# Computing 56 of 96 modulation blocks of a two-model block stack on VectorE instead of TensorE

## The chip, the cores and the metric

The kernel runs on one core of a Trainium2 chip. The metric is the device time in microseconds of one execution; every input and output is float32, and all weights (some 340 MB in one execution) come from HBM. TensorE multiplies, VectorE and ScalarE work element by element, GpSimd helps and starts some transfers, and SyncE's queue starts the loads of the weight stream. In the trace these are PE (with PEld, its weight loads), DVE, ACT, POOL and SP.

## The reference, cut to what matters

The reference is a stack of two layers with adaptive normalisation, followed by a third block (a long convolution, a gated recurrence and a retrieval of experts) that the change doesn't touch. There are 256 tokens of the latent and 256 of the context, width 1024. Each of the two layers begins from modulations, one vector of six times 1024 for the latent's condition and one for the context's:

```python
for i in range(DEPTH):                      # DEPTH = 2
    last = i == DEPTH - 1
    m_lat = (silu(c) @ ada_w[i] + ada_b[i])[:, None, :]     # ada_w[i]: 1024 x 6144
    m_ctx = silu(c_ctx) @ ada_w[i] + ada_b[i]
    sh1, sc1, g1, sh2, sc2, g2 = split(m_lat, 6)
    csh1, csc1, cg1, csh2, csc2, cg2 = split(m_ctx, 6)
    h  = rms(x, norm1_g[i]) * (1 + sc1) + sh1
    hc = rms(y, norm1_g[i]) * (1 + csc1) + csh1
    o, oc = mixer(h, hc)                    # layer 0: Fourier and window attention; layer 1: neighbourhood attention
    x = x + g1 * o
    x = x + g2 * swiglu(rms(x, norm2_g[i]) * (1 + sc2) + sh2)
    if not last:
        y = y + cg1 * oc
        y = y + cg2 * swiglu(rms(y, norm2_g[i]) * (1 + csc2) + csh2)
```

In the last layer the context's rows g1, sh2, sc2 and g2 are used by nothing.

## The kernel before

**The weight stream.** All weights are one list of blocks of 128 x 1024 floats (0.524 MB), in the order in which they are used (`STREAM`). SyncE's queue loads them in that order into a ring of six places (`RING`); a load waits until the block that held its place before is used up. The two 1024 x 6144 matrices of the modulations are 96 such blocks: `ada0a` (16), `ada0b` (32), `ada1a` (16), `ada1b` (32).

**Modulations on TensorE.** `ada` (line 737, its matmul is line 743) takes one block: 128 of the 1024 inputs by 1024 outputs. The condition's column, padded to 32 columns, is the stationary operand and the weight the moving one, in two halves of 512, on 32-column strips of the array, so that the two blocks of a group run side by side. The sums lie in two banks as rows; `ada_copy` (ScalarE) copies them out, and `ada_turn` (TensorE, line 757) turns them into columns with sixteen small matmuls; `mods` (VectorE) adds the bias and forms the gains.

**Where they stand.** `ada0a` opens the program, because the first norm needs it. The others fill TensorE's program elsewhere: `fill[0]`, 48 blocks (`ada0b` and `ada1a`), of which 18 stand between the Fourier steps and 30 in attention 0, two after the scores of each pair; `fill[1]`, 32 blocks (`ada1b`), two after the scores of each of the 16 pairs of attention 1. The turns stand behind the first tile of `ev_out` and of `od_out`, the projections that follow the two attentions.

**An attention** goes over 16 pairs of heads (a pair: two heads, one tile of 128 queries). In step i TensorE's program has scores of pair i (line 949), the two filling blocks, values of pair i-3 (line 970), turning of the probabilities of pair i-2 (line 958). VectorE takes the row minima (`row_min`, line 2168, one instruction that adds the mask and keeps the minimum), ScalarE the exponentials of pair i (line 1593) and behind them in its program the copies of the turned probabilities of pair i-2 (line 1601), GpSimd scales the probabilities (line 2896). Attention 0 has pairs of 512 and of 256 keys, two and two in turn; attention 1 has 512 throughout. In attention 0 GpSimd also splits the four Fourier rows, ahead of its pairs 4 to 7.

**A projection** multiplies in three terms. Each weight block is split in a high part (ScalarE, `high`, line 1612) and a low part (VectorE, `low`, line 2029), both kept in three places (`PARTS`); TensorE does 24 matmuls of 128 x 512 for a tile (line 998). In `ffn`, gate and up tiles alternate: ScalarE applies Silu to gate tile 2m, VectorE multiplies with up tile 2m+1, copies the product's high part and subtracts for its low part. Tile 2m+3 starts once that product has freed its bank (three banks in turn). VectorE's program in step m: low part of block 2m+3, product of pair m, low part of block 2m+4. In `residual` (the end of `ev_out` and `od_out`) VectorE's low parts and residual sums alternate with ScalarE's squares and high parts.

## Time and profile before

| | |
|---|---|
| median of 3 runs | 2174.22 us (2173.36 to 2176.29) |
| the profiled execution | 2173.93 us, its span 2172.1 us |
| TensorE busy | 2100.5 us, 97% of the span |
| VectorE busy | 1399.0 us, 64% |
| ScalarE busy | 973.6 us, 45% |
| GpSimd busy | 321.2 us, 15% |
| matmuls of the modulations (line 743) | 64.9 us busy |
| weight stream | 618 loads of 512 KB by SyncE's queue |

Shares of busy time are averages over stages that have different limits, and a busy TensorE is not one at its peak: its matmuls are pipelined and their ends are modelled. What a stage is bound by is read from the chain of work that ended last (which engine each stretch of the end's history belongs to) and from the timeline of the stage: an engine whose rows stand end to end is the limit there, and a bracket at a row's end names what the engine waited for before it.

### The profile page before, as it was taken

The page shows a single profiled execution, that of the slowest core. Times are in us where ns is not written, and L with a number is a line of the kernel's source. Part 1 is how long each engine was busy: PE and PEld are TensorE (multiplying, and loading weights), DVE is VectorE, ACT ScalarE, POOL GpSimd, SP SyncE. Part 2 cuts the span into 40 slices and gives each one's busy share as a digit, 9 for nine tenths or more (in the row PEclk, how much of TensorE's full clock was granted, in tenths as well). Part 3 has the DMA queues.
Part 4 walks back from the last instruction along what each step waited for, and adds up shares of the span by engine and source line. Part 5 has one row for each costly group of instructions (what it writes and reads, how often), then busy time and mean ns, then how long its engine had stood idle before and what let it go on. Part 6 is the DMA issues. An engine that isn't in the chain of part 4 may idle for free.

```text
span 2172.1 us, 35323 instructions
## 1 busy us (share of the span) xinstructions
PE 2100.5 (97%) x12873; PEld 1777.2 (82%) x12873; DVE 1399.0 (64%) x2524; ACT 973.6 (45%) x1544; POOL 321.2 (15%) x339
## 2 busy tenths in 40 slices
PE   5999999999999999899999999999999999999998
PEld 2754778888878757899999988999988888888887
DVE  4435454443238845665587867997996677777776
ACT  3426332222234345444458635446743444444444
POOL 0014000000003022000000005787840000000000
PEclk9999999999999999999999999999999999999999
DMA  7348322222226356455544634552246655555553
GB/s 287 117 165 312 106 70 97 97 97 97 97 78 175 106 176 205 154 182 183 186 152 175 211 121 140 168 184 68 68 156 219 193 194 187 190 187 192 186 191 116
DMA packets 92751, 341.14 MB, mean 157 GB/s; under 512 B 10367, under 2 KB 10383, under 8 KB 92256
## 3 DMA queue, kind: packets, MB, share of 16 engines
q1 hardware_dynamic: 89280, 325.10, 44.6%
q0 software_dynamic: 3360, 14.51, 2.3%
q8 instruction: 76, 1.25, 0.2%
q14 instruction: 35, 0.29, 0.0%
HBM read 338.52 MB, written 1.05 MB: 156 GB/s over the span
## 4 chain that ended last, share of the span: by engine, by line
PE 89%; DVE 5%; ACT 3%; issue 1%; DMA 1%; SPq 0%; POOL 0%; DVEq 0%; ACTq 0%
PE banks L998 21%; PE banks L1438 16%; PE banks L1047 8%; PE banks L1404 7%; PE banks L1316 6%; PE banks L1187 5%; PE banks L1407 3%; PE banks L1365 3%; PE banks L743 2%; PE banks L923 2%; PE banks L1349 2%; PE banks L1085 2%; PE banks L949 1%; PE banks L970 1%; DMA weight_ring<-in_stream 1%
## 5 line engine op out<-in xcount | busy, mean ns | idle before, releaser
L998 PE MATMUL banks<-act_parts,first_w_parts 128*128 128x512 f32 (+1 forms) x2592 | 477.7, 345 | 7.2 <-DMA small_zone<-in_smalls 3.4
L998 PEld LDWEIGHTS banks<-act_parts,first_w_parts 128*128 128x128 f32 x2592 | 410.4, 190 | 71.0 <-issue 5.6
L2029 DVE TENSOR_TENSOR first_w_parts<-weight_ring,first_w_parts 128x1024 fp32r<-128x1024 f32 x166 | 206.7, 1248 | 263.1 <-ACT first_w_parts L1612 263.1
L1438 PE MATMUL banks<-w_parts,a_parts 128*128 128x512 f32 x1524 | 360.4, 390 | 0.1
L1438 PEld LDWEIGHTS banks<-w_parts,a_parts 128*128 128x128 f32 x1524 | 285.9, 188 | 59.4 <-issue 0.8
L1612 ACT ACTIVATE w_parts<-weight_ring 128x1024 fp32r<-128x1024 f32 x207 | 218.9, 1058 | 184.0 <-PE banks L1404 102.0
L2029 DVE TENSOR_TENSOR w_parts<-weight_ring,w_parts 128x1024 fp32r<-128x1024 f32 x207 | 253.6, 1226 | 72.0 <-ACT w_parts L1612 71.8
L1612 ACT ACTIVATE first_w_parts<-weight_ring 128x1024 fp32r<-128x1024 f32 x166 | 174.7, 1057 | 237.4 <-PE banks L998 125.7
L1404 PE MATMUL banks<-n_parts,w_parts 128*128 128x512 f32 x632 | 229.4, 397 | 1.3 <-DVE w_parts L2029 1.3
L1047 PE MATMUL banks<-ffn_hidden_parts,first_w_parts 128*128 128x512 f32 (+1 forms) x1056 | 183.4, 336 | 0.0
L1047 PEld LDWEIGHTS banks<-ffn_hidden_parts,first_w_parts 128*128 128x128 f32 x1056 | 162.5, 190 | 20.6
L1407 PE MATMUL banks<-n_parts,w_parts 128*128 128x256 f32 x632 | 164.3, 281 | 0.0
L1404 PEld LDWEIGHTS banks<-n_parts,w_parts 128*128 128x128 f32 x632 | 118.6, 188 | 26.8 <-DVE w_parts L2029 1.6
L2029 DVE TENSOR_TENSOR banks<-banks,main_zone 128x256 f32<-128x256 f32 (+1 forms) x174 | 97.7, 565 | 53.4 <-ACT main_zone L1953 52.7
L1407 PEld LDWEIGHTS banks<-n_parts,w_parts 128*128 128x128 f32 x632 | 119.5, 189 | 6.1
L1187 PE MATMUL banks<-n_parts,mix_w_parts 128*128 128x256 f32 (+1 forms) x1008 | 123.2, 284 | 0.5 <-DVE mix_w_parts L2029 0.5
L1187 PEld LDWEIGHTS banks<-n_parts,mix_w_parts 128*128 128x128 f32 x1008 | 122.5, 188 | 0.7 <-DVE mix_w_parts L2029 0.7
L1316 PE MATMUL banks<-n_parts,query_w_parts 128*128 128x256 f32 x888 | 109.9, 284 | 1.9 <-POOL query_w_parts L2934 1.9
L1316 PEld LDWEIGHTS banks<-n_parts,query_w_parts 128*128 128x128 f32 x888 | 107.7, 192 | 2.4 <-POOL query_w_parts L2934 2.3
L2934 POOL TENSOR_TENSOR query_w_parts<-weight_ring,query_w_parts 128x1024 fp32r<-128x1024 f32 x41 | 99.0, 2418 | 51.2 <-ACT query_w_parts L1612 31.4
L2029 DVE TENSOR_TENSOR mix_w_parts<-weight_ring,mix_w_parts 128x1024 fp32r<-128x1024 f32 x59 | 72.0, 1223 | 36.5 <-ACT mix_w_parts L1612 36.1
L1953 ACT ACTIVATE main_zone<-banks 128x256 f32<-128x256 f32 x79 | 30.3, 384 | 124.3 <-PE banks L1404 124.3
(310 smaller groups left out, 2866.5 us busy)
## 6 DMA issues: line engine op xcount, KB each, us to landing
weight_ring<-in_stream SPq DMA_DIRECT2D x618, 512.0 KB, 3.3
main_zone<-in_rel_bias POOLq DMA_DIRECT2D x6, 512.0 KB, 10.9
rounded<-in_dft_input POOLq DMA_DIRECT2D x1, 1600.0 KB, 8.6
rounded<-in_dft_inverse POOLq DMA_DIRECT2D x1, 1280.0 KB, 6.1
main_zone<-in_xT POOLq DMA_DIRECT2D x1, 1024.0 KB, 12.1
main_zone<-in_ctxT POOLq DMA_DIRECT2D x1, 1024.0 KB, 16.9
tail_zone<-in_rel_bias POOLq DMA_DIRECT2D x2, 512.0 KB, 23.7
main_zone<-in_keysT POOLq DMA_DIRECT2D x1, 1024.0 KB, 8.9
```

The lines of the kernel that those rows point to most:

```text
L743: mm = pe.matmul(bank[ADA_BANKS[phase][half]][strip:strip + 32, :], cond[:, k, 10 - 2 * row:42 - 2 * row], wb[:, half * 512:(half + 1) * 512],
L998: mm = pe.matmul(o[:, 0:w], wb[:, hw, k, :], fin[:, hx, k, 0:w], start=(k == 0 and n == 0), stop=(k == DC - 1 and n == 2))
L1047: mm = pe.matmul(o[:, 0:w], wb[:, hw, b % 8, :], fhid[:, hx, k, 0:w], start=(k == 0 and n == 0), stop=(k == FC - 1 and n == 2))
L1187: mm = pe.matmul(o[:, cols], wb[:, hw, k, :], n0p[:, hx, k, cols], start=(k == 0 and n == 0), stop=(k == DC - 1 and n == 2))
L1316: mm = pe.matmul(o[:, 0:L], wb[:, hw, k, :], rows[:, hx, k, :], start=(k == 0 and n == 0), stop=(k == DC - 1 and n == 2))
L1365: mm = pe.matmul(twins[h][:, j * P:(j + 1) * P], one1[:, 8 * h + j, :], one2[:, 8 * h + j, :], start=True, stop=True)
L1404: return pe.matmul(o[:, :], w[:, 0, k, :], n2p[:, :, k, :], start=(k == 0), stop=(k == DC - 1))
L1407: return pe.matmul(o[:, 0:L], w[:, 1, k, :], n2p[:, 0, k, :], start=False, stop=False)
L1438: mm = pe.matmul(acc[n][:, :], ap_[:, e % 3, ha, (n // 2) * P:(n // 2 + 1) * P], wp[(B + b) % PARTS][:, hw, (n % 2) * 512:(n % 2 + 1) * 51 ...
L1612: act.activation(parts[n % PARTS][:, 0, :], slot(s), ACT.Copy).then_inc(w_hi, 1)
L2029: return dve.tensor_tensor(o, a, b, op)
L2934: pool.tensor_tensor(w[:, 1, :], slot(s), w[:, 0, :].bitcast(F32), ALU.subtract).then_inc(w_lo, 1)
```

## The change

`ada0a` stays. `ada0b` is cut to 24 blocks (the rows g1, sh2 and sc2 of layer 0), which stay filling on TensorE: 18 between the Fourier steps and six in the first three pairs of attention 0. The other 56 blocks, row g2 of layer 0 and all of layer 1, become `mods`: each is laid out with the output channel on the partition and all 1024 inputs along the row, and VectorE multiplies it with a row of the condition that is the same on every partition and sums, one instruction for each block and sample (`mod_sums`). The first 24 blocks have two samples (latent and context), the other 32, whose context rows nobody uses, only the latent: 80 instructions. They are woven into the first feed-forward: two blocks in each of the gate and up pairs 1 to 12, five in 13 to 16, four in 17 to 19, one or two (or three) behind each low part, and their blocks stand at the same places of the weight stream. The condition's rows are loaded by GpSimd's queue behind `ev_out`, and ScalarE applies Silu to them behind its first gate tile. The products themselves go to a bank pair that nobody reads. `late_mods` adds biases and forms the gains at the end of gate and up. The turn, the copies and the modulation step of the old `ada1b` are gone.

```diff
-STREAM = [("ada0a", 16), ("ev_in", 10), ("ada0b", 32), ("ada1a", 16), ("ev_out", 8), ("ffn_gu0", 2 * FC), ("ffn_d0", FC),
-          ("od_in", 24), ("ada1b", 32), ("od_out", 8), ("ffn_gu1", 2 * FC), ("ffn_d1", FC),
+STREAM = [("ada0a", 16), ("ev_in", 10), ("ada0b", 24), ("ev_out", 8), ("ffn_gu0", 2 * FC), ("mods", 56), ("ffn_d0", FC),
+          ("od_in", 24), ("od_out", 8), ("ffn_gu1", 2 * FC), ("ffn_d1", FC),
...
+MODS = ([(0, 5, _j, 2) for _j in range(8)] + [(1, _r, _j, 2) for _r in range(2) for _j in range(8)]
+        + [(1, _r, _j, 1) for _r in range(2, 6) for _j in range(8)])
...
+        _c = 1 if _m < 13 else 2 + (_part == 1 and _m < 17)
+        MODS_AT[_m, _part] = range(_at, _at + _c)
...
+                if name == "mods":
+                    return mod_used, n + 1
...
-                nj = [2, 6, 4][phase]
+                nj = [2, 3][phase]
...
-            fill = [[(1, name, b, row0 + b // DC, row0 + b // DC == 0, row0 + b // DC == 5)
-                     for name, n, row0 in (("ada0b", 32, 0), ("ada1a", 16, 4)) for b in range(n)],
-                    [(2, "ada1b", b, b // DC, b // DC == 0, b // DC == 3) for b in range(32)]]
+            fill = [[(1, "ada0b", b, b // DC, b // DC == 0, b // DC == 2) for b in range(24)], []]
...
-                if m == 0:
-                    ada_turn(2)
...
+                    if l == 0 and m == 0:
+                        act.wait_ge(crow_in, 16)
+                        for s in range(2):
+                            act.activation(c_rows[:, s, :], c_rows[:, s, :], ACT.Silu).then_inc(crow_ready, 1)
...
-            ada_copy(2)
...
+            def mod_sums(blocks):
+
+                for b in blocks:
+                    l, row, m, samples = MODS[b]
+                    s = SLOTS["mods"][b]
+                    dve.wait_ge(landed[PLACE[s]], 16 * LOADS[s])
+                    for n in range(samples):
+                        if b == 0:
+                            dve.wait_ge(crow_ready, 2 - n)
+                        last = dve.tensor_tensor_reduce(out=twins[3][:, :], in0=slot(s), in1=c_rows[:, 1 - n, :], scale=1.0, scalar=0.0,
+                                                        op0=ALU.mult, op1=ALU.add, accum_out=MOD[:, l, 8 * row + m, n:n + 1])
+                        if n < samples - 1:
+                            link(last)
+                    last.then_inc(mod_used, 1)
+                    dve.wait_ge(mod_used, b + 1)
...
+                    if l == 0:
+                        mod_sums(MODS_AT.get((m, 0), ()))
                     p = tile(name, 2 * m + 1)[:, 0:w]
...
+                    if l == 0:
+                        mod_sums(MODS_AT.get((m, 1), ()))
+                if l == 0:
+                    late_mods()
...
-            mods(0, 1)
-            mods(1, 0)
+            mods()
             residual("ev_out", 0, 16, T)
...
-            mods(1, 1)
             residual("od_out", 1, 16, L)
...
+            pool.wait_ge(tile_ready, TILE["ev_out"] + 8)
+            pool.dma_start(view(CROWS0, 2 * D), t["c_rows"][:, :]).then_inc(crow_in, 16)
```

What stands in a row on the engines follows, in the line numbers of each kernel. On TensorE in attention 1, a step in the middle before (scores, filling, values, turning of the probabilities):

```order
L949 MATMUL banks<-main_zone 128x512 x2
L743 MATMUL banks<-weight_ring,small_zone 32x512 x4
L970 MATMUL banks<-tail_zone,main_zone 64x128 x8
L958 MATMUL banks<-small_zone,tail_zone 128x128 x8
L949 MATMUL banks<-main_zone 128x512 x2
```

and after:

```order
L968 MATMUL banks<-main_zone 128x512 x2
L989 MATMUL banks<-tail_zone,main_zone 64x128 x8
L977 MATMUL banks<-small_zone,tail_zone 128x128 x8
L968 MATMUL banks<-main_zone 128x512 x2
L989 MATMUL banks<-tail_zone,main_zone 64x128 x8
```

The filling between scores and values is gone; the rest stands in the same order.

On VectorE in gate and up of layer 0, one step before (low part, product, its high and low part, low part):

```order
L2029 TENSOR_TENSOR first_w_parts<-weight_ring,first_w_parts 128x1024 [waits weight_high_parts] x2
L2029 TENSOR_TENSOR banks<-tail_zone,banks 128x512 [waits silu_ready,tile_ready]
L2275 CAST ffn_hidden_parts<-banks 128x512 [waits dve_chain]
L2029 TENSOR_TENSOR ffn_hidden_parts<-banks,ffn_hidden_parts 128x512 [waits dve_chain]
L2029 TENSOR_TENSOR first_w_parts<-weight_ring,first_w_parts 128x1024 [waits weight_high_parts] x2
```

and after, in pair 2 (the instruction of line 2114 multiplies and sums; the short one behind it reads the sum):

```order
L2049 TENSOR_TENSOR first_w_parts<-weight_ring,first_w_parts 128x1024 [waits weight_high_parts,modulation_rows_summed]
L2114 ISA banks,small_zone<-weight_ring,main_zone 128x1024 [waits weights_landed2]
L2114 ISA small_zone 128x1
L2114 ISA banks,small_zone<-weight_ring,main_zone 128x1024 [waits dve_chain]
L2114 ISA small_zone 128x1
L2049 TENSOR_TENSOR banks<-tail_zone,banks 128x512 [waits silu_ready,tile_ready,modulation_rows_summed]
L2323 CAST ffn_hidden_parts<-banks 128x512 [waits dve_chain]
L2049 TENSOR_TENSOR ffn_hidden_parts<-banks,ffn_hidden_parts 128x512 [waits dve_chain]
L2049 TENSOR_TENSOR first_w_parts<-weight_ring,first_w_parts 128x1024 [waits weight_high_parts]
```

Behind each low part stand one block's sums now, and the product waits behind them.

On VectorE at the start of `od_out`, before (low part of block 1, the last modulations, low part of block 2, first residual):

```order
L2029 TENSOR_TENSOR act_parts<-weight_ring,act_parts 128x8x128 [waits weight_high_parts]
L2029 TENSOR_TENSOR small_zone<-banks,small_zone 128x64 [waits ada_ready]
L2022 TENSOR_SCALAR small_zone<-small_zone 128x16 [waits dve_chain]
L2029 TENSOR_TENSOR small_zone<-small_zone 128x16 [waits dve_chain]
L2029 TENSOR_TENSOR unused_query_columns<-weight_ring,unused_query_columns 128x8x128 [waits weight_high_parts,dve_chain]
L2026 SCALAR_TENSOR_TENSOR main_zone<-banks,small_zone,main_zone 128x256 [waits tile_ready]
```

and after (with the last values' high and low part ahead of it):

```order
L2262 CAST act_parts<-banks 128x128 [waits attention_out_ready]
L2049 TENSOR_TENSOR act_parts<-banks,act_parts 128x128 [waits attention_out_high_parts]
L2049 TENSOR_TENSOR act_parts<-weight_ring,act_parts 128x8x128 [waits weight_high_parts]
L2049 TENSOR_TENSOR unused_query_columns<-weight_ring,unused_query_columns 128x8x128 [waits weight_high_parts]
L2046 SCALAR_TENSOR_TENSOR main_zone<-banks,small_zone,main_zone 128x256 [waits tile_ready]
```

The three modulation steps and their wait for the turn have left the place ahead of the low part of block 2.

## Rows read from the trace of the kernel before

**Rows 1.** The page's chain of work that ended last, shares by engine

```profile
PE 89%; DVE 5%; ACT 3%; issue 1%; DMA 1%; SPq 0%; POOL 0%; DVEq 0%; ACTq 0%
```

**Rows 2.** The chain in order of time, gate and up of layer 0: start, us, what

```profile
291.35 228.48 PE banks L998 x1008
```

**Rows 3.** Timeline, TensorE, attention 1: start, us, engine, line, operation, idle before

```profile
786.82 2.08 PE L743 MATMUL banks<-weight_ring,small_zone 128*32 128x512 f32 x8
...
807.29 1.13 PE L949 MATMUL banks<-main_zone 64*128 64x512 f32 x4
808.35 1.06 PE L743 MATMUL banks<-weight_ring,small_zone 128*32 128x512 f32 x8
809.34 1.09 PE L970 MATMUL banks<-tail_zone,main_zone 128*64 128x128 f32 x16
...
811.39 1.13 PE L949 MATMUL banks<-main_zone 64*128 64x512 f32 x4
```

**Rows 4.** Timeline, all engines, same pair: exponentials, then copies of pair i-2

```profile
809.77 0.72 ACT L1593 ACTIVATE tail_zone<-tail_zone,small_zone 128x512 f32<-128x512 f32 x1 [1.62 <-DVE small_zone L2168]
...
811.20 1.05 ACT L1601 ACTIVATE tail_zone<-banks 128x512 f32<-128x512 f32 x2
```

**Rows 5.** Timeline, TensorE, attention 0: a filling, its second half, scores

```profile
168.09 1.05 PE L743 MATMUL banks<-weight_ring,small_zone 128*32 128x512 f32 x4
169.44 1.05 PE L743 MATMUL banks<-weight_ring,small_zone 128*32 128x512 f32 x4 [0.29 <-DMA weight_ring<-in_stream]
...
172.47 1.13 PE L949 MATMUL banks<-main_zone 64*128 64x512 f32 x4
...
187.57 1.13 PE L949 MATMUL banks<-main_zone 64*128 64x512 f32 x4
...
201.44 1.13 PE L949 MATMUL banks<-main_zone 64*128 64x512 f32 x4
```

**Rows 6.** Timeline, all engines, attention 0

```profile
184.37 1.28 POOL L2890 TENSOR_TENSOR act_parts<-main_zone,act_parts 128x512 fp32r<-128x512 f32 x1
...
191.24 1.13 PE L949 MATMUL banks<-main_zone 64*128 64x512 f32 x4
...
194.47 0.70 PE L949 MATMUL banks<-main_zone 64*128 64x256 f32 x4
...
194.79 0.64 ACT L1601 ACTIVATE tail_zone<-banks 128x256 f32<-128x256 f32 x2
...
196.38 0.49 ACT L1593 ACTIVATE tail_zone<-tail_zone,small_zone 128x257 f32<-128x257 f32 x1
```

**Rows 7.** Timeline, start of the od_out stage

```profile
851.54 1.85 PE L757 MATMUL banks<-small_zone,main_zone 128*128 128x8 f32 x16
...
855.25 0.48 DVE L2026 SCALAR_TENSOR_TENSOR main_zone<-banks,small_zone,main_zone 128x256 f32<-128x256 f32 x1
...
858.30 0.48 DVE L2026 SCALAR_TENSOR_TENSOR main_zone<-banks,small_zone,main_zone 128x256 f32<-128x256 f32 x1
```

**Rows 8.** Timeline, start of gate and up of layer 0

```profile
291.20 2.00 ACT L1612 ACTIVATE first_w_parts<-weight_ring 128x1024 fp32r<-128x1024 f32 x2
292.29 1.23 DVE L2029 TENSOR_TENSOR first_w_parts<-weight_ring,first_w_parts 128x1024 fp32r<-128x1024 f32 x1 [5.61 <-ACT first_w_parts L1612]
293.43 0.69 DVE L2029 TENSOR_TENSOR banks<-tail_zone,banks 128x512 f32<-128x512 f32 x1
...
295.55 1.22 DVE L2029 TENSOR_TENSOR first_w_parts<-weight_ring,first_w_parts 128x1024 fp32r<-128x1024 f32 x1
```

**Rows 9.** Groups by line and shape, attention 0: shapes, count | busy, mean ns

```profile
L2168 DVE CUSTOM_DVE_ANT_0 tail_zone<-banks,main_zone,small_zone 128x512 f32<-128x512 f32 x12 | 8.9, 747 | 0.0
...
L2168 DVE CUSTOM_DVE_ANT_0 tail_zone<-banks,main_zone,small_zone 128x256 f32<-128x256 f32 x16 | 7.6, 478 | 0.0
```

**Rows 10.** Timeline, VectorE in the norm ahead of gate and up of layer 1

```profile
882.41 0.48 DVE L2026 SCALAR_TENSOR_TENSOR act_parts<-main_zone,small_zone,act_parts 128x256 fp32r<-128x256 f32 x1
```

**Rows 11.** Stretches, attention 0: us; busy by engine; granted clock, DMA share, GB/s

```profile
170.00:175.00 5.00, 5.00 (x48) 2.65 (x46) 1.88 (x7) 1.52 (x3) 0.32 (x1) 1.00 0.98 373
```

More of the change, by code:

```diff
@@ L67 @@
           ("peer", 2 * KEYS - DONE)]
-SLOT = {}
+MODS = ([(0, 5, _j, 2) for _j in range(8)] + [(1, _r, _j, 2) for _r in range(2) for _j in range(8)]
+        + [(1, _r, _j, 1) for _r in range(2, 6) for _j in range(8)])
+MODS_AT = {}
 _at = 0
-for _n, _c in STREAM:
-    SLOT[_n] = _at
-    _at += _c
-NSLOTS = _at
+for _m in range(1, 20):
+    for _part in range(2):
+        _c = 1 if _m < 13 else 2 + (_part == 1 and _m < 17)
+        MODS_AT[_m, _part] = range(_at, _at + _c)
+        _at += _c
+assert _at == len(MODS)
+ORDER = []
+for _n, _c in STREAM:
+    for _i in range(_c if _n != "mods" else 0):
+        ORDER.append((_n, _i))
+        if _n == "ffn_gu0" and _i >= 3:
+            ORDER += [("mods", _b) for _b in MODS_AT.get(((_i - 3) // 2, (_i - 3) % 2), ())]
+SLOTS = {_n: [] for _n, _ in STREAM}
+for _s, (_n, _i) in enumerate(ORDER):
+    SLOTS[_n].append(_s)
+SLOT = {_n: _s[0] for _n, _s in SLOTS.items()}
+NSLOTS = len(ORDER)
 SPLIT = ("ev_in", "ev_out", "ffn_gu0", "ffn_d0", "od_in", "od_out", "ffn_gu1", "ffn_d1", "w_in2a", "w_in2b", "w_in2c", "w_in2d",
@@ L79 @@
 KIND = []
-_n = [0, 0]
-for _name, _c in STREAM:
-    _k = _name in SPLIT
-    ORD[_name] = _n[_k]
-    for _i in range(_c):
-        KIND.append((_k, _n[_k], _name, _i))
-        _n[_k] += 1
+_n = [0, 0, 0]
+for _name, _i in ORDER:
+    _k = 2 if _name == "mods" else int(_name in SPLIT)
+    ORD.setdefault(_name, _n[_k])
+    KIND.append((_k, _n[_k], _name, _i))
+    _n[_k] += 1
 EARLY_QUERIES = 4
@@ L237, in ada_strip @@
     return (2 * k + k // 4 % 2) % 4 ^ half
+CROWS0 = 21504
 HALF0 = FS0 + 2048
@@ L3112, in layout @@
         ada = x["ada_w"][l].reshape(DC, P, 6, 1024).transpose(2, 0, 1, 3).reshape(48, P, 1024)
-        parts[f"ada{l}a"], parts[f"ada{l}b"] = ada[:16], ada[16:]
+        if l == 0:
+            parts["ada0a"], parts["ada0b"] = ada[:16], ada[16:40]
         parts[f"ffn_gu{l}"] = woven(tiled(x["ffn_w_gate"][l]), tiled(x["ffn_w_up"][l]))
         parts[f"ffn_d{l}"] = tiled(x["ffn_w_down"][l])
+    parts["mods"] = np.stack([x["ada_w"][l][:, D * row + P * m:D * row + P * (m + 1)].T for l, row, m, _ in MODS])
     stream = np.empty((NSLOTS, P, 1024), np.float32)
```

47 lines of the change are left out of this document (29 added, 18 removed).

## The prediction

> **What bounds the kernel now.** I read the chain of work that ended last first: 89% of it is TensorE, the rest short stretches of VectorE, ScalarE and DMA [rows 1]. So an edit pays only where it shortens TensorE's program, or a stretch where TensorE waits. The first gate and up projection is TensorE alone: 42 tiles in one unbroken piece, 228.48/42 = 5.44 us a tile [rows 2]. In the two attentions TensorE's own timeline shows, for every pair of heads, scores, the two modulation blocks as filling, values of three pairs ago, turning of two pairs ago, with nothing between [rows 3]. There too TensorE is the bound, but what the filling hides has to be looked up: in the timeline of all engines, ScalarE starts the exponentials 2.48 us after the scores start and ends the copies of the turned probabilities 4.96 us after [rows 3, 4]. Those are on no path today, and are next when the filling goes.
>
> **Removed: the filling of attention 1** (32 blocks, two in each of 16 pairs). A pair takes 811.39 - 807.29 = 4.10 us, of which the filling is 809.34 - 808.35 = 0.99 [rows 3]. Without it TensorE alone would need 3.11. But values of pair i-2, which stand in pair i+1, need the copies of pair i-2, and ScalarE does these behind the exponentials of pair i. Count from scores i: copies done at +4.96 [rows 4], about +0.09 for the semaphore (estimate), then values and turning, 811.39 - 809.34 = 2.05 [rows 3], and after them come scores i+2. Two pairs per 7.10 us are 3.55 a pair. The gain is therefore 0.55 of the 0.99, in the 13 pairs from the fourth on: 7.1 us. The first three have no values to do, their scores wait for VectorE's minima, and I give them nothing. One filling there took 2.08 where the others take 1.06 [rows 3], because its weights were late: another 1.0. Sum 8.1 us. Ends: 13 x 0.99 + 1.0 = 13.9 if ScalarE kept up, and 1.0 if the chain took all of it back.
>
> **Removed: the filling of attention 0 from the fourth pair on** (24 of 30 blocks; pairs 0 to 2 keep theirs). Sizes alternate there, two pairs of 512 keys, two of 256, so I take rounds of four: 201.44 - 187.57 = 13.87 us [rows 5]. The same reasoning, with this attention's offsets: after scores of 512 keys the copies start at 194.79 - 191.24 = +3.55, after scores of 256 at 196.38 + 0.49 - 194.47 = +2.40; copies of 256 take 0.64 [rows 6], of 512 1.05 [rows 4]; values and turning take about 0.59 each for 256 (estimate: half of 1.03 and a fixed part). Following the even pairs: (3.55 + 0.64 + 0.08 + 0.59 + 0.59) + (2.40 + 1.05 + 0.08 + 1.03 + 1.02) = 11.0; the odd ones: (3.55 + 0.64 + 0.08 + 0.59 + 1.02) + 5.36 (TensorE's own work there) = 11.2. The slower sets it: 13.87 - 11.2 = 2.65 a round, and 12 fillings are three rounds: 8.0 us. Late weights go as well: the filling that began at 168.09 should have let the next scores start at 168.09 + 1.0 + 2.05 = 171.1, and they started at 172.47, its second half having waited for a DMA: 1.3; the round behind it took 187.57 - 172.47 = 15.10, 1.2 over the clean one [rows 5]. Against this GpSimd splits the Fourier rows in pairs 4 to 7, one subtraction of 1.28 and more for each [rows 6]; at the new pace it is nearly full, and I charge 0.5 (between 0 and 1.3). Sum 10.0 us. Ends: 12 x 1.0 + 2.5 = 14.5, and 2.5.
>
> **Removed: the turn of the last modulations in the od_out stage.** VectorE there waits for tile 0, then for TensorE's sixteen small matmuls of the turn (they start at 851.54, where tile 0 ends), then does three links and a weight's low part before the first residual at 855.25 [rows 7]. From there a ladder of VectorE and ScalarE runs, 858.30 - 855.25 = 3.05 us a step, longer than TensorE's tile; whoever starts the ladder earlier ends it earlier. With the turn gone the low part needs nothing new and is done while tile 0 runs, and the residual can start 0.14 behind 851.54: 855.25 - 851.68 = 3.6; I take 3.5. In the ev_out stage the turn stays, TensorE is the bound, and the three links that leave VectorE there are worth nothing.
>
> **Added: 80 multiply-and-sum instructions on VectorE in the gate and up projection.** 24 blocks have two samples and 32 one. The form, both inputs in SBUF and 1024 long, is in no row. The nearest are the attention's row minima, the same instruction with one input in PSUM: 0.478 us for 256, 0.747 for 512 [rows 9], so 0.269 for each further 256, and 0.747 + 2 x 0.269 = 1.28 for 1024. With reading the sum and waiting for itself I take 1.35 apart (estimate). Per gate-and-up pair VectorE does today two low parts at 293.43 - 292.29 = 1.14 and three steps of the product, 295.55 - 293.43 = 2.12 [rows 8]: 4.4 of TensorE's 10.88. Pairs 1 to 12 get four sums: 4.4 + 5.4 = 9.8. Pairs 13 to 16 get five: 11.15, which is 0.27 too long, four times 1.1. Pairs 17 to 19 have four again. What stands behind a late sum on VectorE is the next product; TensorE's tile 2m+3 needs its bank one tile after that product's input is ready, so it can be 5.44 - 2.1 - 0.1 = 3.2 late. 1.1 is below this: cost 0. From the fixed parts, the sums begin to cost at (10.88 - 4.4)/4 = 1.62 apart.
>
> **Added on the other queues.** ScalarE gets two Silu of 1024 before the high part of block 3. Its rows of that size take 1.0 each [rows 8]. That block's low part stands ahead of the first product on VectorE, which now ends near 297.7 instead of 295.6, and tile 3 would start at 291.2 + 5.44 = 296.6: cost 1.1, once, and 0 to 3. SP loads 100 blocks instead of 44 through the same six places; the densest stretch is seven in 10.88 us, 7 x 0.524 MB/10.88 = 337 GB/s, and five microseconds of attention 0 moved 373 [rows 11]. It fits, without much left; cost 0, at worst a few us. The row load of the condition is on GpSimd's queue, which has nothing else there. The seven small links at the end of the projection lie ahead of low parts that are three blocks early.
>
> **The sum.** 10.0 + 8.1 + 3.5 - 1.1 = 20.5 us. The profiled execution took 2173.93; 2173.93 - 20.5 = 2153.4. The median of the runs is 0.3 above the profiled one: 2153.7.
>
> **A rule against it.** The row that bears on the price is a scalar-tensor-tensor with both inputs in SBUF, 256 long and without a sum: 0.48 us [rows 10], as long as the minima of that length, so two SBUF inputs alone halve nothing here. The Trainium skill, Vector Engine (DVE) Microarchitecture Reference, section 7 "Points that are easy to get wrong", says of a related instruction form that two SBUF sources wider than bf16 halve its throughput, because no read port is left for the accumulator. No run here shows a form that both sums and reads twice from SBUF, so it stands as a rival.
>
> **Rivals.**
> - The sums run at half rate. Slope doubled, 0.21 + 4 x 0.54 = 2.36, and 2.43 apart. Then VectorE bounds the projection: 4.4 + 9.7 = 14.1 in fifteen pairs (3.2 over) and 16.6 in four (5.7 over), 48 + 23 - 3 = 68 us. 2153.7 + 68 = 2222, slower. It decides from about 1.83 apart, where the loss, 60 x (1.83 - 1.62) + 20 x (1.83 - 1.30) - 3.2, eats the 20.5. For it: no row shows the form. Against: the row above. 0.12.
> - The sums are somewhat dearer, 1.65 to 1.8 apart, or weights come late where seven blocks share a pair: 5 to 18 us back, 2159 to 2172. 0.11.
> - ScalarE's chain does not bind: attentions fall to TensorE's own pace, 13.9 + 14.5 + 3.5 - 1.1 = 30.8: 2143. Against: its copies stand behind the exponentials in program order. 0.07.
> - The change does little: the chains take the filling's time back, only stalls and the turn are left, 1.0 + 2.5 + 3.5 - 1.1 = 5.9: 2168. Against it: ScalarE's own work in a pair, from the first exponential to the last copy, is 812.25 - 809.77 = 2.48 [rows 4], far from 4.10. 0.04.
> - My forecast, 2147 to 2160: 0.66.
>
> **How the numbers follow.** A measurement of this kernel can tell about 0.2%, 4.3 us, from no change. The range 2143 to 2172 takes in all but the half rate and tails, some 0.16. Faster by over 0.2% (below 2169.9): the forecast, the better case, and most of the dearer sums and of the little-gain case, 0.80. Within 0.2%: 0.06. Slower: the half rate and worse mishaps, 0.14.
>
> **What would show it.** The sums' row: 1.28 confirms the price, above 1.6 fails it. The projection's TensorE piece: unbroken but for a gap of about 1 us at tile 3. In attention 1, scores alternating at about 3.1 and 4.0 us with TensorE waiting for ScalarE's copies; regular 3.1 would make the second attention's term too small, 4.1 none at all. In the od_out stage the first residual right behind tile 0. The forecast is wrong if VectorE is busy all through the projection while TensorE waits for its low parts or banks.

## The result, and the profile after

The changed kernel takes 2157.18 us (median of four runs, 2156.76 to 2157.65) where the kernel before, on the same chip, takes 2173.86 (2173.36 to 2176.29): a ratio of 0.9924, 95% interval 0.9911 to 0.9938. The profiled execution took 2157.02, its span 2155.2. The forecast was 2153.7 with 2143 to 2172, and faster. Profile against profile the gain is 16.9 us where 20.5 was forecast. I take it apart by stage, each from TensorE's first matmul in it to its first in the next; the columns are the kernel before, the changed one, the difference and the forecast term.

| stage | before | after | difference | forecast |
|---|---|---|---|---|
| start to attention 0 | 159.96 | 158.34 | -1.6 | none |
| attention 0 | 61.18 | 51.95 | -9.2 | -10.0 |
| ev_out | 55.17 | 55.17 | 0 | 0 |
| gate and up, layer 0 | 243.36 | 244.53 | +1.2 | +1.1 |
| down, layer 0 | 119.77 | 119.77 | 0 | 0 |
| norm, od_in, values' rows | 137.89 | 138.91 | +1.0 | 0 |
| attention 1 | 71.23 | 64.91 | -6.3 | -8.1 |
| od_out and its norm | 33.68 | 31.90 | -1.8 | -3.5 |
| the rest | 1289.86 | 1289.72 | -0.1 | 0 |

(The gate and up projection is 0.16 us longer, in both, if counted to the start of the next piece in the chain, as the expectations below do.)

The page's chain by engine answers [rows 1]; TensorE's share is 88% where it was 89%, ScalarE's 4% where it was 3%.

```profile
PE 88%; DVE 5%; ACT 4%; issue 2%; DMA 1%; POOL 0%; SPq 0%; DVEq 0%; ACTq 0%
```

**Gate and up** first. The chain in order of time (start, us, what) answers [rows 2] and [rows 8]:

```profile
281.31 1.05 ACT main_zone L1659
282.36 0.96 ACT first_w_parts L1629
...
283.37 1.11 issue
...
284.48 0.70 DVE banks L2049
...
286.00 0.70 DVE ffn_hidden_parts L2049
...
286.83 223.32 PE banks L1017 x984
```

The second Silu of the condition (L1659), block 3's high part, its low part (VectorE runs it in the 1.11 us that the chain calls issue), the product: then tile 3, for which TensorE waited 0.89 us, and from there TensorE is unbroken for 223.32 us. The sums are one row of the page (busy us, mean ns of one | idle before):

```profile
L2114 DVE CUSTOM_DVE_ANT_0 banks<-weight_ring,main_zone 128x1024 f32<-128x1024 f32 x80 | 98.4, 1230 | 1.4
```

1.23 us each, 98.4 us of VectorE's time, and the only place where they show in the stage's length is that Silu.

**Attention 1.** TensorE's timeline (start, us, engine, line, operation, idle before) at its start and in the steady part answers [rows 3]:

```profile
768.67 1.13 PE L968 MATMUL banks<-main_zone 64*128 64x512 f32 x4 [0.78 <-ACT main_zone L1591]
...
771.18 2.42 PE L968 MATMUL banks<-main_zone 64*128 64x512 f32 x4 [1.38 <-DVE small_zone L2214]
...
774.53 2.48 PE L968 MATMUL banks<-main_zone 64*128 64x512 f32 x4 [0.93 <-DVE small_zone L2214]
...
776.94 1.83 PE L977 MATMUL banks<-small_zone,tail_zone 128*128 128x128 f32 x8
...
778.70 1.13 PE L968 MATMUL banks<-main_zone 64*128 64x512 f32 x4
...
796.64 1.13 PE L968 MATMUL banks<-main_zone 64*128 64x512 f32 x4
...
801.67 1.09 PE L989 MATMUL banks<-tail_zone,main_zone 128*64 128x128 f32 x16 [0.73 <-ACT tail_zone L1618]
...
803.72 0.70 PE L968 MATMUL banks<-main_zone 64*128 64x512 f32 x2
```

In the steady part two pairs take 803.72 - 796.64 = 7.08 us, and every second time the values (L989) wait 0.73 for ScalarE's copies. That is the loop the prediction named, at its 7.10. At the start, though, the scores of pairs 1 and 2 last 2.42 and 2.48 us and the turning 1.83, and scores one to four start at 0, 2.51, 5.86 and 10.03 us of the stage. In the kernel before, these scores took 1.53 and 1.52, the turning 1.09, and scores started at 0, 2.50, 4.96 and 8.43:

```profile
777.33 1.13 PE L949 MATMUL banks<-main_zone 64*128 64x512 f32 x4 [0.78 <-ACT main_zone L1574]
...
779.83 1.53 PE L949 MATMUL banks<-main_zone 64*128 64x512 f32 x4 [0.38 <-DVE small_zone L2168]
...
782.29 1.52 PE L949 MATMUL banks<-main_zone 64*128 64x512 f32 x4
...
784.74 1.09 PE L958 MATMUL banks<-small_zone,tail_zone 128*128 128x128 f32 x8
785.76 1.13 PE L949 MATMUL banks<-main_zone 64*128 64x512 f32 x4
```

The stretches of the changed kernel point to the reason (us; busy by engine; granted clock, DMA share, GB/s):

```profile
768.00:771.00 3.00, 1.13 (x4) 0.33 (x4) 1.06 (x5) 1.81 (x2) 0.00 (x0) 1.00 0.02 5
771.00:774.00 3.00, 2.42 (x4) 0.74 (x4) 1.32 (x9) 1.52 (x4) 0.00 (x0) 0.61 0.00 0
774.00:777.00 3.00, 2.47 (x5) 0.97 (x6) 1.38 (x10) 1.52 (x4) 1.36 (x2) 0.50 0.00 0
```

The granted clock falls to 0.50 there, the lower of TensorE's two levels, 1.2 instead of 2.4 GHz. In the kernel before, the same pairs ran at 1.00 (from its stretches):

```profile
780.00:783.00 3.00, 3.00 (x15) 1.17 (x16) 1.96 (x12) 2.06 (x7) 0.18 (x1) 1.00 0.54 178
```

**Attention 0.** TensorE's scores at the head of two rounds of four pairs, which answer [rows 5]:

```profile
169.22 1.13 PE L968 MATMUL banks<-main_zone 64*128 64x512 f32 x4
...
181.14 1.13 PE L968 MATMUL banks<-main_zone 64*128 64x512 f32 x4
...
192.51 1.13 PE L968 MATMUL banks<-main_zone 64*128 64x512 f32 x4
```

11.37 us for the clean round (forecast 11.2), 11.92 for the one in which GpSimd splits the Fourier rows (0.55 more; 0.5 was charged).

**od_out.** VectorE's timeline answers [rows 7]: residuals (L2046) of tiles 0, 1, 5, 6 and 7; between the last two, left out here, stand three low parts of the next projection:

```profile
836.76 0.49 DVE L2046 SCALAR_TENSOR_TENSOR main_zone<-banks,small_zone,main_zone 128x256 f32<-128x256 f32 x1 [0.55 <-PE banks L1132]
...
839.82 0.48 DVE L2046 SCALAR_TENSOR_TENSOR main_zone<-banks,small_zone,main_zone 128x256 f32<-128x256 f32 x1
...
852.03 0.48 DVE L2046 SCALAR_TENSOR_TENSOR main_zone<-banks,small_zone,main_zone 128x256 f32<-128x256 f32 x1
...
854.04 0.48 DVE L2046 SCALAR_TENSOR_TENSOR main_zone<-banks,small_zone,main_zone 128x256 f32<-128x256 f32 x1 [1.53 <-PE banks L1132]
...
859.37 0.48 DVE L2046 SCALAR_TENSOR_TENSOR main_zone<-banks,small_zone,main_zone 128x256 f32<-128x256 f32 x1
```

The first residual comes 3.18 us after the stage began, 3.5 earlier than before, as forecast, and the step is still 3.06. But at tile 6 the ladder stands 1.53 us waiting for TensorE. Before, the residual of tile 6 followed that of tile 5 without a wait (one row of two) and the last one came 5.33 us behind it, as it does now:

```profile
870.51 0.87 DVE L2026 SCALAR_TENSOR_TENSOR main_zone<-banks,small_zone,main_zone 128x256 f32<-128x256 f32 x2
...
876.23 0.47 DVE L2026 SCALAR_TENSOR_TENSOR main_zone<-banks,small_zone,main_zone 128x256 f32<-128x256 f32 x1
```

Counted from the start of the stage, the last residual stands at 25.79 us now and at 27.67 before: 1.88 earlier, the whole gain of the stage.

### The profile page after: what moved, and what is told of

It reads as the page before. It is cut to its first block, busy times and chain, and to the rows that moved or that the text cites. A ratio compares the mean times of both kernels' runs of the same rounds, so it can differ in the third digit from the quotient of the medians.

```text
span 2155.2 us, 34722 instructions
## 1 busy us (share of the span) xinstructions
PE 2072.6 (96%) x12633; PEld 1772.2 (82%) x12633; DVE 1500.0 (70%) x2685; ACT 974.8 (45%) x1544; POOL 322.9 (15%) x340
## 3 DMA queue, kind: packets, MB, share of 16 engines
HBM read 339.57 MB, written 1.05 MB: 158 GB/s over the span
## 4 chain that ended last, share of the span: by engine, by line
PE 88%; DVE 5%; ACT 4%; issue 2%; DMA 1%; POOL 0%; SPq 0%; DVEq 0%; ACTq 0%
PE banks L1017 21%; PE banks L1455 16%; PE banks L1066 8%; PE banks L1421 7%; PE banks L1333 6%; PE banks L1204 5%; PE banks L1424 3%; PE banks L1382 3%; PE banks L942 2%; PE banks L1366 2%; PE banks L1104 2%; PE banks L1217 1%; PE banks L968 1%; PE banks L1031 1%; PE banks L1132 1%
## 5 line engine op out<-in xcount | busy, mean ns | idle before, releaser
L2114 DVE CUSTOM_DVE_ANT_0 banks<-weight_ring,main_zone 128x1024 f32<-128x1024 f32 x80 | 98.4, 1230 | 1.4
```

Of the source, the lines that this page charges most:

```text
L2114: last = dve.tensor_tensor_reduce(out=twins[3][:, :], in0=slot(s), in1=c_rows[:, 1 - n, :], scale=1.0, scalar=0.0, op0=ALU.mult, op1=ALU.a ...
```

## The experiments

Nine kernels, each an edit of the changed one. Their stages, in us, from one profile each, beside the median of the runs where there was more than one (the profiled execution can lie some us from it: 2153.09 for `warm_four`, 2150.75 for `best`):

| kernel | start | attention 0 | ev_out | gate, up | norm to values' rows | attention 1 | od_out | total |
|---|---|---|---|---|---|---|---|---|
| changed | 158.34 | 51.95 | 55.17 | 244.53 | 138.91 | 64.91 | 31.90 | 2157.18 |
| sums_short | 159.32 | 51.98 | 55.18 | 244.51 | 138.62 | 66.04 | 31.39 | 2157.32 |
| sums_six | 159.39 | 51.50 | 55.21 | 274.43 | 139.71 | 66.16 | 31.64 | 2188.4 (one run) |
| silu_late | 162.29 | 52.03 | 55.17 | 243.34 | 138.65 | 66.05 | 31.49 | 2159.4 (one run) |
| od_delay | 158.89 | 51.62 | 55.22 | 244.49 | 138.61 | 66.03 | 31.37 | 2156.9 (one run) |
| filled | 159.79 | 58.77 | 55.21 | 244.51 | 138.74 | 70.23 | 33.79 | 2171.06 |
| warm3 | 160.22 | 51.84 | 55.19 | 244.53 | 138.16 | 64.59 | 30.93 | 2157.29 |
| warm_four | 157.91 | 51.93 | 55.18 | 244.50 | 138.63 | 63.32 | 31.79 | 2158.21 |
| copies_first | 159.78 | 51.30 | 57.69 | 244.52 | 137.98 | 59.12 | 31.80 | 2152.80 |
| best | 161.54 | 50.41 | 55.22 | 243.33 | 139.25 | 57.62 | 31.81 | 2147.89 |

The table also shows what one execution can tell: where the code is the same, the start scatters over 4 us, the stage from the norm to the values' rows over 1.7, attention 1 over 1.3 (64.91 to 66.16, five profiles), attention 0 over 0.5 (51.50 to 52.03) and od_out over 1.0 (30.93 to 31.90). The untouched gate and up scatters over 0.04.

### Are the sums free?

Two theories: they lie in VectorE's idle time, or they delay something without a visible gap. First the sums over 8 elements, which leaves out nearly all of each.

```diff
-dve.tensor_tensor_reduce(out=twins[3][:, :], in0=slot(s), in1=c_rows[:, 1 - n, :], ...
+dve.tensor_tensor_reduce(out=twins[3][:, 0:8], in0=slot(s)[:, 0:8], in1=c_rows[:, 1 - n, 0:8], ...
```

> The 80 sums of the changed kernel run over 8 elements instead of 1024; their loads, waits and places stay. It leaves out nearly all of each sum, so its modulations are not the reference's. Theory: the sums lie in VectorE's idle time of the first gate and up projection and cost nothing, so the stage from its first matmul to the start of the down projection stays at 244.70 us (within 0.2) and the total at 2157 (within 2); VectorE is busy some 90 us less. Rival: the sums delay products or low parts without a visible gap in TensorE's row, so the stage shortens by 1 us or more; it can't shorten below 243.52, what it took before the change.

The stage stayed at 244.51, the total at 2157.32 (ratio to before 0.993, 0.9913 to 0.9946). The sums are free. The group of their line (duration min/median/max in ns, first and last start in us) gives the price too, in the changed kernel and in this one:

```profile
L2114 DVE CUSTOM_DVE_ANT_0 banks<-weight_ring,main_zone x80: 1225/1232/1236, 289.6 to 493.4; 128x1024 f32<-128x1024 f32 x80
...
L2114 DVE CUSTOM_DVE_ANT_0 banks<-weight_ring,main_zone x80: 165/174/176, 290.6 to 493.4; 128x8 f32<-128x8 f32 x80
```

(1232 - 174)/1016 = 1.04 ns an element, where the minima with one input in PSUM cost 0.269/256 = 1.05 [rows 9]. So both inputs in SBUF and a sum together cost nothing extra. The halving by two SBUF sources that the Trainium skill states of a related form (Vector Engine (DVE) Microarchitecture Reference, section 7 "Points that are easy to get wrong") does not show in this instruction: 1.23 us measured, where half rate, by the prediction's estimate, would have been 2.36.

Then how much room was left: two more sums in each pair.

```diff
-                    for n in range(samples):
+                    todo = [0] * (b == blocks[0]) + list(range(samples))
+                    for at, n in enumerate(todo):
...
-                        if n < samples - 1:
+                        if at < len(todo) - 1:
                             link(last)
```

> The changed kernel with the first sum of every call made twice: 118 sums instead of 80, six in most gate-and-up pairs and seven in four of them, each to the same place, so the result stays. Theory: a sum takes 1.23 us and stands 1.32 from the next; VectorE has 1.15 us left in a pair of 10.88, so each of 15 pairs goes 1.5 over and each of four 2.8, less 3.2 of slack: the stage from first matmul to the down projection grows by about 30 us, to some 275, the total to some 2187, with TensorE waiting for VectorE's low parts. Rival: VectorE has more room than its row shows (its instructions overlap or the slack of the weights' parts renews itself in each pair): under 15 us.

The stage grew by 29.9 us. TensorE waits in it for the product's low part, which frees the product's bank (us in total, times, longest), and VectorE's low parts of weights stand one pair apart at:

```profile
PE banks L1017 <- DVE ffn_hidden_parts L2049: 26.0, 18, 2.6
```

```profile
301.44 1.23 DVE L2049 TENSOR_TENSOR first_w_parts<-weight_ring,first_w_parts 128x1024 fp32r<-128x1024 f32 x1
...
313.78 1.23 DVE L2049 TENSOR_TENSOR first_w_parts<-weight_ring,first_w_parts 128x1024 fp32r<-128x1024 f32 x1
```

These are 12.34 us, VectorE without a pause: 4.4 for its old work and six times 1.32. So the prediction's account of VectorE's time holds beyond its edge too: by it, at four sums of 1.32 VectorE has 1.2 us of a pair's 10.88 left and is not the bound.

### Does the Silu make the gap at tile 3?

```diff
-                    if l == 0 and m == 0:
-                        act.wait_ge(crow_in, 16)
-                        for s in range(2):
-                            act.activation(c_rows[:, s, :], c_rows[:, s, :], ACT.Silu).then_inc(crow_ready, 1)
                     for b in (2 * m + 3, 2 * m + 4):
                         if b < 2 * FC:
                             high(name, b)
...
+                        if l == 0 and m == 0 and b == 3:
+                            act.wait_ge(crow_in, 16)
+                            for s in range(2):
+                                act.activation(c_rows[:, s, :], c_rows[:, s, :], ACT.Silu).then_inc(crow_ready, 1)
```

> The changed kernel with ScalarE's two Silu of the condition's rows put one place later, behind the high part of block 3 instead of ahead of it. Theory: these two of 1.0 us each made block 3's high part, its low part behind VectorE's product, and so TensorE's tile 3 late, by the 0.89 us for which TensorE waits at 286.83; now tile 3 follows without a wait and the stage from first matmul to the down projection takes about 243.6 instead of 244.70 us, nearly the 243.52 of before the change. The first sums, one pair later, don't wait. Rival: the wait comes from the product's bank, or moves to a later tile with the first sums: still 244.5 or more.

243.34: the 1.2 us are gone, the stage is as long as before the change (243.36), and TensorE runs through tile 3 from 284.35 on while the Silu follow the high part. The rival falls.

```profile
284.35 9.91 PE L1017 MATMUL banks<-act_parts,first_w_parts 128*128 128x512 f32 x43
...
284.37 1.05 ACT L1629 ACTIVATE first_w_parts<-weight_ring 128x1024 fp32r<-128x1024 f32 x1
...
285.32 2.00 ACT L1664 ACTIVATE main_zone<-main_zone 128x1024 f32<-128x1024 f32 x2
```

### Is the gain the filling's time?

All removed TensorE work, put back with zeros and without loads, and od_out's three links on VectorE with it; the sums stay.

```diff
...
+def idle_fill(l, i):
+    zeros = view(CS_0 + 12, 32)
+    rows = V[l][:, 0, 0:4, :] if l else V[l][:, :, 0, :]
+    for n in range(2):
+        for half in range(2):
+            strip = 32 * ada_strip((2 * i + n) % DC, half)
+            mm = pe.matmul(bank[6 + half][strip:strip + 32, :], zeros, rows, start=bool(l), stop=l == 1 or i > 12)
...
                             ada(*f)
+                        if i >= 3 - 3 * l and i < 15 + l:
+                            idle_fill(l, i)
...
+                if m == 0:
+                    for k in range(DC):
+                        mm = pe.matmul(bank[7][:, 8 * k:8 * k + 8], V[1][:, 0, 0, :], small("pick")[:, 0:8], start=True, stop=True)
+                    mm.then_inc(ada_ready, 1)
...
             attention(1)
+            dve.wait_ge(ada_ready, 2)
+            link(tt_(att[:, 0, 0, 0:64], bank[7][:, 0:64], att[:, 0, 1, 0:64], ALU.add))
+            gains(1, 1, 1)
             residual("od_out", 1, 16, L)
```

> The changed kernel with all that was removed put back as TensorE work without loads: four matmuls of zeros, the shape of two blocks, behind the scores of pairs 3 to 14 of the first attention and of every pair of the second, on four different strips of 32 columns of the array as the blocks had them, and in the od_out stage sixteen small matmuls behind tile 0 with three links of VectorE that wait for them. The sums stay. Theory: the fillings' time comes back without the late weights: second attention 64.9 to about 70.2 us (71.23 before, less the 1.0 that waited for a load), first attention 51.95 to about 58.7 (61.18 less 2.5), od_out stage 31.90 to 33.7; total about 2171. So the sums and their loads, which stay, are worth less than 2 us of the whole difference. Rival: the gain came from the loads that moved, and fillings without loads fit into TensorE's waits: under 6 us in all, 2163 or less.

58.77, 70.23 and 33.79 against 58.7, 70.2 and 33.7; the total is 2171.06, which can't be told from the kernel before (ratio 1.0001, 0.9992 to 1.0011). So by stages the gain is the time of the removed TensorE work and of its late loads, and the 80 sums with their 56 loads cost nothing there but the Silu's 1.2. By the total this is less sharp: without late loads (3.4) and with the Silu this kernel should be 2.2 faster than the one before, and that lies at the edge of the interval, so a cost of up to some 2 us outside these stages isn't excluded. The run also splits the attentions' terms, from one profile each. Late weights were worth 61.18 - 58.77 = 2.4 and 71.23 - 70.23 = 1.0 (forecast 2.5 and 1.0); the filling itself 6.8 and 5.3 (forecast 7.5 and 7.1).

### What is missing in attention 1?

The theory was the clock; the rival, that minima or exponentials hold the first pairs back. Zeros behind the scores of the first three pairs:

```diff
...
+                        if l == 1 and i < 3:
+                            idle_fill(l, i)
```

> The changed kernel with four matmuls of zeros (128x32 stationary, 512 moving, the shape of two removed modulation blocks, no weights to load) put back behind the scores of the first three pairs of the second attention, 12 in all. Theory: there TensorE stands idle without the filling and its granted clock falls to 0.50 to 0.61 between 771 and 777 us, where it was 1.00 before the change; with something to do the clock stays at 1.00, scores one to four start at 0, 2.5, 5.0 and 8.4 as before the change instead of 0, 2.5, 5.9 and 10.0, and the stage shortens by about 1.6 us (64.91 to 63.3). Rival: the later starts come from VectorE's minima or ScalarE's exponentials and not from the clock: then the added matmuls change nothing or cost up to their own 3 us, and the total rises.

The clock stayed at 1.00 in those pairs, but the stage took 64.59 and the total didn't move. This first form put two of the four matmuls on each of two strips, and they took 1.91 us, too long to be hidden: scores started at 0, 2.90, 5.81 and 9.73.

```profile
770.77 1.91 PE L957 MATMUL banks<-main_zone,small_zone 128*32 128x512 f32 x8
```

The second form put them on four strips, in the two banks as well, as the removed blocks were, with the loop of `filled`'s `idle_fill`.

> The changed kernel with the four matmuls of zeros behind the scores of the first three pairs of the second attention on four different strips of 32 columns of the array and over two banks, as the removed blocks stood, where the earlier run with zeros used two strips twice and took 1.91 us for four. Theory: four take 1.06 us and fit into the wait for VectorE's minima, so the first scores start at 0, 2.5, 5.0 and 8.4 us as before the change, with a granted clock of 1.00; what the second attention lacks to the forecast is the clock alone, and the stage takes about 63.1 us (71.23 less the forecast 8.1; 64.59 with the slower zeros, 64.91 to 66.16 in the five profiles without zeros there and with the same code). Rival: part of the shortfall is in the steady pairs or at the end: 64 or more.

```profile
767.92 1.13 PE L977 MATMUL banks<-main_zone 64*128 64x512 f32 x4 [0.78 <-ACT main_zone L1602]
...
768.98 1.06 PE L958 MATMUL banks<-main_zone,small_zone 128*32 128x512 f32 x8
...
770.42 1.52 PE L977 MATMUL banks<-main_zone 64*128 64x512 f32 x4 [0.38 <-DVE small_zone L2225]
...
772.88 1.53 PE L977 MATMUL banks<-main_zone 64*128 64x512 f32 x4
...
776.36 1.13 PE L977 MATMUL banks<-main_zone 64*128 64x512 f32 x4
```

Scores start at 0, 2.50, 4.96 and 8.44, to a hundredth as before the change (0, 2.50, 4.96, 8.43), and the stage takes 63.32, 1.27 less than with the first form, which is what its fourth scores were later (1.29). So the clock accounts for 1.6 us against the changed kernel's profile, and for 2.7 against the other four profiles without zeros, in which the low clock lasted longer. The total doesn't show it: 2158.21 (2153.09 to 2159.05), a ratio of 0.9942 (0.9926 to 0.9959). A stage's 1.6 us is below what these runs can tell, and I don't call the zeros a gain.

### Is the ladder still the bound in od_out?

An idle addition on VectorE, 1.23 us, behind its wait for tile 0:

```diff
 b = tile(name, m)
+if l == 1 and m == 0:
+    tt_(att[:, 0:2, 0, 0:512], att[:, 0:2, 0, 0:512], att[:, 0:2, 1, 0:512], ALU.add)
```

> The changed kernel with one idle addition of 1024 elements a row (about 1.2 us) put on VectorE between its wait for tile 0 of the od_out stage and the first residual, so that the ladder of residuals, ScalarE's high parts and low parts starts 1.2 us later. Theory: the ladder is no longer the bound of this stage; it stands 1.53 us waiting for TensorE's tile 6 at 854.04, so a start 1.2 later costs nothing and only that wait shrinks to about 0.3: the stage (start of od_out to first matmul of gate and up) stays at 31.9 within 0.3. Rival, the prediction's own step: whoever starts the ladder later ends it later, 33.1.

```profile
837.80 1.23 DVE L2049 TENSOR_TENSOR tail_zone<-tail_zone 128x1024 f32<-128x1024 f32 x1 [0.55 <-PE banks L1132]
...
838.94 0.48 DVE L2046 SCALAR_TENSOR_TENSOR main_zone<-banks,small_zone,main_zone 128x256 f32<-128x256 f32 x1
...
855.08 0.48 DVE L2046 SCALAR_TENSOR_TENSOR main_zone<-banks,small_zone,main_zone 128x256 f32<-128x256 f32 x1 [0.40 <-PE banks L1132]
...
860.41 0.48 DVE L2046 SCALAR_TENSOR_TENSOR main_zone<-banks,small_zone,main_zone 128x256 f32<-128x256 f32 x1
```

The wait at tile 6 shrank from 1.53 to 0.40, and the last residual stands 25.78 us behind the start of the stage (834.63), where it stood at 25.79: a ladder that starts 1.2 later ends no later. So ahead of tile 6 the ladder has 1.5 us to spare, and TensorE's row of tiles up to there is the bound. The stage as a whole took 31.37, shorter than the expected 31.9 within 0.3. That difference, like the whole scatter of this column (30.93 to 31.90, leaving out `filled`), lies behind the last residual, in the norm, where the profiles differ in the granted clock: from 857 to 862 and from 862 to 866 us it was 0.84 and 0.50 in the changed kernel's and 1.00 and 0.67 in that of `warm3`, the shortest.

### Does the copies' place close the loop?

ScalarE's copies of pair i-2 ahead of the exponentials of pair i:

```diff
 for i in range(PAIRS + 2):
...
-    if i < PAIRS:
...
-            act.activation(e, e, ACT.Exp, bias=stat[:, 1, u:u + 1], scale=-1.0, accum_out=stat[:, 2, u:u + 1]).then_inc(exp_ready, 1)
     j = i - 2
     if 0 <= j < PAIRS:
...
             act.activation(att_pt[:, j % 2, half, 0:n], bank[2 + half][:, 0:n * P].rearrange("p (k n) -> p k n", k=n),
                            ACT.Copy).then_inc(pt_copied, 1)
+    if i < PAIRS:
...
+            act.activation(e, e, ACT.Exp, bias=stat[:, 1, u:u + 1], scale=-1.0, accum_out=stat[:, 2, u:u + 1]).then_inc(exp_ready, 1)
```

> The changed kernel with ScalarE's copies of the turned probabilities of pair i-2 put ahead of the exponentials of pair i in its program, in both attentions. Theory: the loop of two pairs in 7.07 us is closed by the copies standing behind the exponentials; ahead of them they end about 3.8 us after scores i start, before the values that need them (4.2), and pairs fall to TensorE's own 3.1 us each: 13 pairs by 0.43, about 5.5 us off the second attention (64.91 to 59.4). In the first attention TensorE's own work is about 9.9 a round of four where 11.4 is shown, but GpSimd splits rows in pairs 4 to 7: 2 to 4 us off (51.95 to about 49). Total about 2149. Rival: the exponentials, now later, make VectorE's reciprocals, GpSimd's scaling and the turning late, and the loop only changes its place: within 2 us of 2157, or slower.

Attention 1 took 59.12 (59.4 expected): from the fifth pair on one pair every 3.11 us, TensorE without a pause, ScalarE now waiting for it:

```profile
795.58 1.13 PE L968 MATMUL banks<-main_zone 64*128 64x512 f32 x4
...
798.36 1.08 ACT L1611 ACTIVATE tail_zone<-banks 128x512 f32<-128x512 f32 x2 [0.62 <-PE banks L977]
...
798.68 1.13 PE L968 MATMUL banks<-main_zone 64*128 64x512 f32 x4
```

So the place of the copies in ScalarE's program was the loop. In attention 0 I was wrong: 51.30, 0.65 less instead of 2 to 4, with a scatter of 0.5. The clean round fell to 192.82 - 182.20 = 10.62, but the other stayed near 11.9, and at the end the two high parts stood ahead of the copies of pair 14. And ev_out, which I had not thought of, grew by 2.5: its tile 0 took 8.25 us instead of 5.74, at the lower clock again.

```profile
208.00:212.00 4.00, 2.76 (x20) 1.85 (x17) 3.26 (x6) 1.66 (x5) 0.00 (x0) 0.71 0.14 41
212.00:216.00 4.00, 4.00 (x11) 3.03 (x11) 0.16 (x1) 1.03 (x1) 0.00 (x0) 0.50 0.62 221
```

The total was 2152.80 where 2149 was expected, ratio 0.9915 (0.9899 to 0.9932). This interval overlaps the changed kernel's (0.9911 to 0.9938), so the totals don't show a gain over it; the stages above make 3.9 us.

### A version from these

Copies ahead, with one of the two high parts before and one behind the copies of pair 14; the zeros on four strips; the Silu one place later.

```diff
-    if l == 0 and i == PAIRS:
-        for b in range(PARTS - 1):
-            high("ev_out", b, None, owp)
...
+    if i == PAIRS:
+        high("ev_out", 0, None, owp) if l == 0 else high_out(0)
     j = i - 2
     if 0 <= j < PAIRS:
...
+    if i == PAIRS:
+        high("ev_out", 1, None, owp) if l == 0 else high_out(1)
...
```

> Three edits in one on the changed kernel: ScalarE's copies ahead of the exponentials in both attentions, with the first two high parts of the next projection around the copies of the last pair but one instead of both ahead of them; matmuls of zeros on four different strips behind the scores of the first three pairs of the second attention; the rows' Silu behind block 3. Theory: the second attention takes about 57.6 us (59.1 with the copies ahead alone, less 0.6 for a clock that stays at 1.00 and 0.9 for the end), the first about 50.4 (51.3 less 0.9), tile 0 of ev_out goes back from 8.25 to 5.74 since TensorE idles less ahead of it, and gate and up loses its gap of 0.9: total about 2147, 10 below the changed kernel. Rival: TensorE still idles enough at the end of the first attention for the clock to fall in ev_out, and the zeros cost what the clock gives: 2150 to 2152.

50.41 and 57.62 in the attentions, ev_out at 55.22, gate and up at 243.33: each stage as expected. The total is 2147.89 (2147.35 to 2150.75), a ratio of 0.9894 (0.9878 to 0.9911) to before, 23.4 us below the runs of before beside it. The changed kernel was 16.7 below its own; so the version gains some 6.7 us over it, with intervals that just touch, where 10 were expected.

## Why the prediction was right, point by point

- **What bounds.** TensorE, with a next bound behind the filling: held, and `filled` shows no other gain in these stages.
- **The sums at no cost.** Held. 1.23 us each (1.28 estimated), 1.32 apart (1.35), with no more room than the account says (`sums_six`). The half-rate rival falls by the sums' row (1.23, not 2.36) and by `sums_short`.
- **ScalarE's Silu, +1.1.** Measured +1.2, at the tile named, and gone when moved.
- **Attention 0, -10.0.** Measured -9.2. Late weights 2.4 for 2.5, GpSimd 0.55 for 0.5; the pace term was too large by 0.65, of which the three rounds, at 11.37 and not 11.2, make 0.5; the rest is within what one profile can tell.
- **Attention 1, -8.1.** The mechanism and its size in the steady pairs held (7.08 for 7.10). The failed step is "the first three have no values to do ... and I give them nothing": nothing gained was right in program terms, but they lost 1.6 us and more, because TensorE, which waits there, was granted the lower clock. Measured -6.3, and -7.9 with the clock held up by zeros.
- **od_out, -3.5.** Measured -1.8. The failed step is "whoever starts the ladder earlier ends it earlier". The ladder did start 3.5 earlier; but TensorE's eight tiles of 2.9 us, 23.2 in all, ran without a break before too, except for the turn, so without it they end only 1.9 us earlier. The residual of tile 6 waits for its tile, and the last one follows it by 5.33 as before: 1.88 gained, and what the ladder gained beyond that it stands waiting. Before, the two met at tile 6: TensorE went on from it 22.09 us into the stage, and its residual followed at 22.34. I had compared step with tile (3.05 against 2.9), and not the ladder's five steps to tile 6 (first residual to the residual of tile 5, 852.03 - 836.76 = 15.3) with TensorE's six tiles there (17.3).
- **The size.** The four stages that the change touches gave 9.2 + 6.3 + 1.8 - 1.2 = 16.1 us of the forecast 20.5. That the profiles differ by 16.9 is owed to the scatter below, which gave back 0.7 by chance.
- **Terms that weren't there.** The start's -1.6 and the +1.0 between the down projection and attention 1 need no cause in the change: over the ten kernels above they scatter by 4.4 and 1.7 with the same code. Part of the second is the clock: TensorE's first unbroken stretch of od_in, some 20 us behind the start of that stage, ran at a granted 0.78 in the changed kernel's profile and at 1.00 in that of before (the two rows below, in this order). What makes the start scatter stays open.

```profile
650.00:655.00 5.00, 5.00 (x33) 4.89 (x32) 2.45 (x2) 3.31 (x7) 5.00 (x9) 0.78 0.76 155
```

```profile
660.00:665.00 5.00, 5.00 (x41) 4.89 (x40) 2.45 (x2) 4.37 (x10) 5.00 (x8) 1.00 0.80 163
```

## What to carry to other kernels

Work that fills a busy engine's program is worth only the distance to the next bound behind it, so find that bound's loop in the timeline and measure its period before counting the filling's time as gain; here 0.55 of 0.99 us a pair, and the rest came by moving one engine's two steps past each other. Ahead of a ladder of several engines compare the whole ladder to a tile with the whole row of tiles, not step with step. And where TensorE will wait, look up the granted clock that it had while it was kept busy: the pairs right behind may run at half of it.

## What the runs showed of the hardware that I had not expected

- TensorE's granted clock fell to 0.50 in a stage in which it still worked in every pair: in the changed kernel after 1.13 us of work in 3 us, with no wait longer than 1.38 us behind the first scores, and it stayed low through some 7 us (some 10 in the profiles of `sums_short`, `sums_six`, `silu_late` and `od_delay`, some 3 in that of `copies_first`). It isn't one execution's whim there: the six profiles without filling in those pairs all show it, the five with blocks or zeros (before, `filled`, `warm3`, `warm_four`, `best`) show 1.00. The Trainium skill, TensorE: Matmul & The Clock Gate, section "Why this matters for your kernels", advises against long idle gaps between bursts of matmuls. Here there was no long one, and the clock fell all the same, behind waits of 0.78 and 1.38 us on either side of the first scores. In ev_out it is less certain: in the one profile of `copies_first`, with a wait of 1.73 us among the last values of attention 0, it fell (8.25 us for a tile); in those of the changed kernel and of `best`, with 0.76 and 0.78 there, it didn't.
- Four matmuls with a 32-column stationary operand took 1.06 us on four different strips of the array and 1.91 us on two strips used twice. So the filling's price depended on where its outputs stood.
